# Attention sums with P as the fixed operand, and log-sum loads inside the attention stage

## What is computed

```python
s = jnp.einsum('bnqhd,bnkhd->bnhqk', qb, kk)      # 128 queries x (previous block, own block) of keys
s = jnp.where(mask[None, :, None], s, -jnp.inf)
m = jnp.max(s, axis=-1, keepdims=True)
p = jnp.exp(s - m)
den = jnp.sum(p, axis=-1, keepdims=True)
o = jnp.einsum('bnhqk,bnkhd->bnqhd', p / den, vv)
lse = (m + jnp.log(den))[..., 0]
...
w = jax.nn.softmax(jnp.stack(lses, axis=0), axis=0)   # over the three groups
comb = jnp.einsum('gbsh,gbshd->bshd', w, o)
```

## Time and profile before

| what | us |
|---|---|
| median of 3 runs | 2387.86 (2382.49 to 2400.88) |
| the profiled execution | 2381.88 |
| its span, first to last instruction | 2380.1 |
| TensorE busy | 2281.7 (96%) |
| VectorE busy | 1699.8 (71%) |
| ScalarE busy | 805.8 (34%) |

### The profile page before, as it was taken

One profiled execution on the slowest core, in us unless ns is written; L12 is line 12 of the kernel. 1 busy time (PEld: TensorE's weight loads), 2 busy tenths in 40 slices (PEclk: granted clock), 3 DMA queues, 4 the chain that ended last, 5 costly groups with the idle time before them and its releaser, 6 DMA issues. The chain is left out here.

```text
span 2380.1 us, 36205 instructions
## 1 busy us (share of the span) xinstructions
PE 2281.7 (96%) x12996; PEld 1840.0 (77%) x12996; DVE 1699.8 (71%) x3313; ACT 805.8 (34%) x1705; POOL 299.4 (13%) x487
## 2 busy tenths in 40 slices
PE   7999999979999999999999999889999899999998
PEld 5788878767788888888878887668778636888887
DVE  6756668757685688888868887788888758556663
ACT  5332222112224422121122233776777524122121
POOL 1000012212210012222221210111111000000000
PEclk9999999999999999999999999999999999999999
DMA  8999999999996667878787888766555397434431
GB/s 263 254 278 333 280 276 271 258 248 272 289 276 211 205 190 225 276 253 276 240 264 226 264 293 300 226 228 204 166 192 177 127 319 297 186 117 162 165 146 65
DMA packets 271184, 553.40 MB, mean 233 GB/s; under 512 B 33392, under 2 KB 60480, under 8 KB 268896
## 3 DMA queue, kind: packets, MB, share of 16 engines
q1 hardware_dynamic: 200688, 358.77, 44.2%
q0 software_dynamic: 58000, 166.36, 26.9%
q10 hardware_dynamic: 12320, 25.96, 3.0%
HBM read 442.60 MB, written 191.50 MB: 266 GB/s over the span
## 5 line engine op out<-in xcount | busy, mean ns | idle before, releaser
L1663 PE MATMUL b_acc<-b_whi,a_hi 128*128 128x512 f32 x1792 | 707.0, 395 | 14.9 <-DVE b_wlo L1319 7.3
L1664 PE MATMUL b_acc<-b_wlo,a_hi 128*128 128x512 f32 x1792 | 701.4, 391 | 0.0
L1665 PE MATMUL b_acc<-b_whi,a_lo 128*128 128x512 f32 x1792 | 701.3, 391 | 0.0
L1069 ACT CAST b_whi<-b_w 128x2048 fp32r<-128x2048 f32 (+1 forms) x127 | 228.8, 1802 | 528.3 <-PE b_acc L1665 369.2
L1663 PEld LDWEIGHTS b_acc<-b_whi,a_hi 128*128 128x128 f32 x1792 | 338.9, 189 | 88.8 <-issue 9.4
L1665 PEld LDWEIGHTS b_acc<-b_whi,a_lo 128*128 128x128 f32 x1792 | 338.6, 189 | 71.2
L1664 PEld LDWEIGHTS b_acc<-b_wlo,a_hi 128*128 128x128 f32 x1792 | 339.0, 189 | 69.2
L1319 DVE TENSOR_TENSOR b_wlo<-b_w,b_whi 128x2048 fp32r<-128x2048 f32 (+1 forms) x127 | 273.1, 2151 | 92.2 <-ACT b_whi L1069 92.1
L1113 ACT ACTIVATE c_sm<-c_sm,c_ends 128x256 f32<-128x256 f32 (+1 forms) x384 | 172.5, 454 | 16.6 <-DVE c_ends L1467 16.1
L1467 DVE CUSTOM_DVE_ANT_0 c_sm<-c_p_s,c_mask 128x256 f32<-128x256 f32 (+1 forms) x384 | 120.4, 361 | 36.6 <-PE c_p_s L1752 35.3
L981 POOL DMA_DIRECT2D a_x<-tm x188 | 108.1, 586 | 259.0 <-DVE sT L1433 182.0
(11 more groups left out here) (374 smaller groups left out, 3491.3 us busy)
## 6 DMA issues: line engine op xcount, KB each, us to landing
b_w<-t SPq DMA_DIRECT2D x64, 1024.0 KB, 8.0
t<-in_w_in POOLq DMA_DIRECT2D x48, 1024.0 KB, 11.2
b_w<-in_w_in SPq DMA_DIRECT2D x47, 1024.0 KB, 7.8
a_x<-tm POOLq DMA_DIRECT2D x167, 256.0 KB, 7.1
tm<-b_st SPq DMA_DIRECT2D x128, 256.0 KB, 7.3
b_ck<-in_cache_kv_w POOLq DMA_DIRECT2D x96, 256.0 KB, 4.8
c_qk<-tm SPq DMA_DIRECT2D x96, 256.0 KB, 3.3
t<-t POOLq DMA_DIRECT2D x16, 1024.0 KB, 12.7
```

The costliest lines, as they stand in the source:

```text
L1069: nc.scalar.copy(whi[:, b % HI_RING, part, 0:w], w_raw[:, k, part, 0:w]).then_inc(w_hi, 1)
L1663: nc.tensor.matmul(out, stat_hi, mov_hi, start=first, stop=False)
L1664: nc.tensor.matmul(out, stat_hi, mov_lo, start=False, stop=False)
L1665: return nc.tensor.matmul(out, stat_lo, mov_hi, start=False, stop=last)
```

## The change

`sums` takes P's transpose (128 keys x 128 queries) as the fixed operand and V's 64 columns of the head as the moving one. The output of a task then has queries in the partitions and the 8 heads' 512 columns in a row; `p_o` is [128, 512]. ScalarE copies it to `og` directly. `oT`, `o_move` and the transposes back are gone. `ends_copy` stays at its step, `o_store` moves to the same step. Eleven of the twelve `load_lse` go from SP's list behind the attention into its loop over steps, seven steps after the last unit's scores of the tasks concerned (two steps more for each further load of the two groups whose tasks finish early), each after a wait for the store; the twelfth stays.

```diff
-        p_o = pb("c_p_o", [P, 4, P])
+        p_o = pb("c_p_o", [P, CH])
...
+                lse_at = {}
+                for g in range(3):
+                    of = [i for i, x in enumerate(tasks) if x.g == g]
+                    for n in range(3 if g == 0 else 4):
+                        last = of[4 * n + 3] if g == 0 else of[-1]
+                        lse_at.setdefault(last_unit(last).q // 2 + 7 + (2 * n if g else 0), []).append((g, 4 * n, last))
...
+                    for g, t, last in lse_at.get(s, ()):
+                        for k in range(2):
+                            sp.wait_ge(og_out[k], 16 * ((last - k) // 2 + 1))
+                        late_lse(g, t)
...
-                    if i >= 1:
-                        act.wait_ge(o_moved, i)
-                    nc.scalar.copy(oT[:, :, :], p_o[:, :, :]).then_inc(o_evacd, 1)
+                    if i >= 2:
+                        act.wait_ge(og_out[i % 2], 16 * (i // 2))
+                    nc.scalar.copy(og[:, i % 2, 0:CH], p_o[:, :]).then_inc(o_evacd, 1)
...
-                    act.wait_ge(o_moved, i + 1)
+                    act.wait_ge(o_evacd, i + 1)
...
-                    if q in turn_o_at:
-                        ends_copy(turn_o_at[q])
-                    if q - 2 in turn_o_at:
-                        o_store(turn_o_at[q - 2])
+                    if q - 2 in sum_at and sum_at[q - 2][1].c == 3:
+                        ends_copy(sum_at[q - 2][1].i)
+                        o_store(sum_at[q - 2][1].i)
...
-                def o_move(i):
-                    dve.wait_ge(tqk_done, tqk_no[i, 2])
-                    if i >= 2:
-                        dve.wait_ge(og_out[i % 2], 16 * (i // 2))
-                    V.tensor_copy(og[:, i % 2, 0:CH], p_qk[:, :]).then_inc(o_moved, 1)
...
-                    for b in ((1,) if near else (0, 1)):
-                        n = x.i if b else tasks[x.i].prev
-                        for h in range(2):
-                            cols = slice((2 * x.c + h) * HD, (2 * x.c + h + 1) * HD)
-                            last = nc.tensor.matmul(p_o[HD * h:HD * (h + 1), x.c, :], v[:, n % KEPT, cols],
-                                                    pT[:, x.u % 2, 2 * h + b, :], start=(b == 1 if near else b == 0),
-                                                    stop=(b == 1))
+                    for h in range(2):
+                        cols = slice((2 * x.c + h) * HD, (2 * x.c + h + 1) * HD)
+                        for b in ((1,) if near else (0, 1)):
+                            n = x.i if b else tasks[x.i].prev
+                            last = nc.tensor.matmul(p_o[:, cols], pT[:, x.u % 2, 2 * h + b, :], v[:, n % KEPT, cols],
+                                                    start=(b == 1 if near else b == 0), stop=(b == 1))
...
-                    if q in turn_o_at:
-                        transposes(turn_o_at[q], 2)
...
-        def load_lse():
-            for t in range(0, NT, 4):
-                for g in range(3):
-                    sp.dma_start(lse[:, t:t + 4, g, :], OG[:, g, CH:].rearrange("(t p) c -> p t c", p=P)[:, t:t + 4, :]
-                                 ).then_inc(lse_in, 16)
+        def load_lse(g, t):
+            sp.dma_start(lse[:, t:t + 4, g, :], OG[:, g, CH:].rearrange("(t p) c -> p t c", p=P)[:, t:t + 4, :]
+                         ).then_inc(lse_in, 16)
...
-            load_lse()
+            load_lse(0, NT - 4)
```

More of the change, by code:

```diff
@@ L212, in plan_phase @@
         sb("m_weights", [P, (160160 - 147872) // 4])
-        B["og"], B["ends"], B["oT"] = sb("c_og", [P, 2, OG_W]), sb("c_ends", [P, 4, 2 * NH]), sb("c_oT", [P, 4, P])
+        B["og"], B["ends"] = sb("c_og", [P, 2, OG_W]), sb("c_ends", [P, 4, 2 * NH])
     return B
@@ L450, in project @@
     turn_q_at = {units[4 * i].q - 6: i for i in range(N_TASK)}
-    turn_o_at = {units[4 * i].q + 8: i for i in range(N_TASK)}
     turn_kd_at = {at + 2: n for n, at in t_at.items()}
-    turn_at = sorted((q, place, (i, a)) for a, place, of in ((1, 5, turn_k_at), (0, 5, turn_q_at), (2, 1, turn_o_at),
-                                                          (3, 3, turn_kd_at)) for q, i in of.items())
+    turn_at = sorted((q, place, (i, a)) for a, place, of in ((1, 5, turn_k_at), (0, 5, turn_q_at), (2, 3, turn_kd_at)) for q, i in of.items())
     tqk_no = {what: n + 1 for n, (_, _, what) in enumerate(turn_at)}
-    turned_first = {what: [sum(1 for i, a in tqk_no if a == kind and tqk_no[i, a] < n) for kind in range(4)]
+    turned_first = {what: [sum(1 for i, a in tqk_no if a == kind and tqk_no[i, a] < n) for kind in range(3)]
                     for what, n in tqk_no.items()}
@@ L479, in project @@
         key_of = lambda u: early_keys[key_at[u]] if u < units_early else ck[:, key_at[u], :]
-        qk, v, qT, kT, sm, pT, og, ends, oT = [B[k] for k in ("qk", "v", "qT", "kT", "sm", "pT", "og", "ends", "oT")]
+        qk, v, qT, kT, sm, pT, og, ends = [B[k] for k in ("qk", "v", "qT", "kT", "sm", "pT", "og", "ends")]
         sb("m_projection", [P, (186656 - 24992) // 4])
@@ L540, in project @@
         pt_done, pv_done, o_evacd, o_turned = sem("c_pt_done"), sem("c_pv_done"), sem("c_o_evacd"), sem("c_o_turned")
-        pt_evacd, o_moved = [sem("c_pt_evacd_act"), sem("c_pt_evacd_dve")], sem("c_o_moved")
+        pt_evacd = [sem("c_pt_evacd_act"), sem("c_pt_evacd_dve")]
         turns_ = sem("c_turns")
@@ L554, in attention_over @@
             eng.wait_ge(o_turned, N_TASK)
-            eng.wait_ge(o_moved, N_TASK)
+            eng.wait_ge(o_evacd, N_TASK)
             for k in range(2):
@@ L853, in _ @@
                     block_load_at.setdefault(form_over[n % NFORM], []).append(k)
-                SP_END = max(LATE // 2 + 6, *qk_load_at, *v_load_at) + 1
-                late_tail, late_tile, late_main = ending.sync(sp)
+                lse_at = {}
[4 more added lines that the diff above has]
+                        lse_at.setdefault(last_unit(last).q // 2 + 7 + (2 * n if g else 0), []).append((g, 4 * n, last))
+                SP_END = max(LATE // 2 + 6, *qk_load_at, *v_load_at, *lse_at) + 1
+                late_tail, late_tile, late_main, late_lse = ending.sync(sp)
                 sp.dma_start(lnw[:, :], A["ln_w"]).then_inc(const_in, 16)
@@ L1165, in kd_evac @@
                 def kd_evac(n):
-                    act.wait_ge(tqk_done, tqk_no[n, 3])
+                    act.wait_ge(tqk_done, tqk_no[n, 2])
                     if n >= 1:
@@ L1576, in attend @@
                 def attend(q):
-                    for x in score_at.get(q, ())[0:1]:
-                        mask_and_max(x)
-                    if q in turn_o_at:
-                        o_move(turn_o_at[q])
-                    for x in score_at.get(q, ())[1:2]:
+                    for x in score_at.get(q, ()):
                         mask_and_max(x)
@@ L1715, in transposes @@
                 def transposes(i, a):
-                    for done, n in zip((q_evacd, k_evacd, o_moved, kd_evacd), turned_first[i, a]):
+                    for done, n in zip((q_evacd, k_evacd, kd_evacd), turned_first[i, a]):
                         if n:
@@ L1720, in transposes @@
                         pe.wait_ge(h_dve, N_CONV)
-                    if a == 3:
+                    if a == 2:
                         pe.wait_ge(keyed_g, i + 1)
@@ L1725, in transposes @@
                     else:
[L1726 to L1729, removed]
+                        pe.wait_ge(qk_in[i % 2], 32 * (i // 2) + 32)
                         for c in range(4):
-                            y = oT[:, c, :] if a == 2 else qk[:, i % 4, a, c * P:(c + 1) * P]
-                            last = nc.tensor.transpose(p_qk[:, c * P:(c + 1) * P], y, ident[:, :])
+                            last = nc.tensor.transpose(p_qk[:, c * P:(c + 1) * P], qk[:, i % 4, a, c * P:(c + 1) * P], ident[:, :])
                     last.then_inc(tqk_done, 1)
@@ L1858, in attend @@
                     if q in turn_kd_at:
-                        transposes(turn_kd_at[q], 3)
+                        transposes(turn_kd_at[q], 2)
                     for x in turn_p_at.get(q, ()):
@@ L1905, in _ @@
                     attend(q)
-                pe.wait_ge(o_moved, N_TASK)
+                pe.wait_ge(o_evacd, N_TASK)
                 late_main()
@@ L2292, in main @@
                 sp.wait_ge(stored[k], 16 * (len(range(k, TILES, 2)) + (k == LAST % 2)))
-        return tail, tile, main
+        return tail, tile, main, load_lse
     def gpsimd(pool):
```

## The result

| kernel | median, us | ratio to the kernel before |
|---|---|---|
| before | 2387.86 (2381.27 to 2400.88, 7 runs) | 1 |
| after | 2411.36 (2406.82 to 2416.59, 7 runs) | 1.009 [1.0068, 1.0111] |

The change makes the kernel slower by 0.9%: +21.5 us by the ratio, +23.5 by the medians. The middle is just under 1%; the interval reaches from 0.7 to 1.1%, so these runs do not settle on which side of 1% the change lies. The forecast was 2401 us with a range of 2381 to 2422: the time lies inside, 10 us above it.

The account below looks back on a forecast made before the run. TensorE was taken to bound the attention stage nearly one for one, except in four gate stretches. 67.6 - 27.8 - 9.6 - 12 - 5 = +13.2 us on 2387.9 gave 2401 us, range 2381 to 2422.

Parts of the forecast that it names:

- P fixed, V moving: Attention sums on TensorE: 1200 instructions go from 0.0547 to 0.111 us each, +67.6 us; lower bound +18.4.
- tile shape: Between sums and P's transposes: same shape now, so 0.1 us less at each of 96 bursts, -9.6 us.
- The row of the recurrence's products: Profile row of matmuls with 128 fixed, 64 moving columns, 0.110 us each; taken as pace for the new sums.
- rival (A): Attention sums: moving columns alone set the pace, 0 to +18.4 us, say +9; kernel faster at 2360 us; chance 0.13.
- Turning back: Attention, between scores and sums: four transposes per task vanish, 48 x 0.58 us, -27.8 us.
- those stretches: Four parts of the attention stage where gate blocks load VectorE and ScalarE; TensorE idles 24.8 us there.
- Waits that shrink: Four gate stretches of attention: TensorE waits less for scores' minima and exponentials, -12 us, bounds 0 and -25.
- Log-sum loads: SP's queue behind attention: eleven of twelve loads move into the loop, -5 us, bounds 0 and -12.
- Rival (B): Gate stretches: TensorE's waits stay and the late stage gives nothing, +30.2 us, 2418 us; chance 0.24.
- its own line: Test for the rival of staying waits: it decides once waits and log-sum loads together give less than 6.3 us.
- its own bound of 25: Attention stage: 15 to 20 us growth expected; growth over 25 us would mean wrong in the main.

Follow-up runs that it names:

- E4: Changed kernel with each product of the sums moving 128 columns of V instead of 64; 2407.03 us, 1.0075 of the kernel before.
- E3: Changed kernel with V's columns fixed again and outputs stored turned, the turning back left out of the computation; 2372.04 us, 0.9934 of the kernel before.
- E2: Kernel before with eleven log-sum loads moved into the attention loop, sums as they were; 2380.98 us, 0.9967 of the kernel before.
- E1: Changed kernel with all twelve log-sum loads behind the attention, as before the change; 2418.78 us, 1.0124 of the kernel before.
- E9: Changed kernel with VectorE's and ScalarE's five wide gate operations per block cut to 64 of 512 columns; 2389.52 us, 1.0038 of the kernel before.
- E10: Kernel before with eleven log-sum loads moved and both engines' wide gate operations cut to 64 of 512 columns; 2360.67 us, 0.9908 of the kernel before.
- E8: Changed kernel with only VectorE's five wide gate operations per block cut to 64 of 512 columns; 2405.81 us, 1.0078 of the kernel before.

## Why the prediction was right in its class and 10 us low

- **P fixed, V moving: +67.6 us, right by its pace.** The sums' loads last 192 ns (190 expected), 16 of them take 2.00 us (1.9). From the first sum to P's transposes it is 1710.92 - 1709.08 = 1.84 us, where it was 1704.17 - 1703.14 = 1.03: +0.81 a burst of 16, and the terms for pace and tile shape give 16 x 0.0563 - 0.1 = 0.80. The row of the recurrence's products was the right neighbour, and E4 shows what rival (A) disputed: 64 or 128 moving columns, the pace is the same. Of the Trainium skill, "TensorEngine Tiling (Array Packing)", section "When to Use Tiling", the runs agree with the rule that a fixed operand of at most 64 columns should be packed: from E3 to the changed kernel, packed to unpacked, the runs grow by 37 us.
- **Turning back -27.8, tile shape -9.6: right as work, wrong as time by themselves.** TensorE's busy time falls by 23.1 us in E3 and the intervals of 0.2 and 0.1 us between bursts came as forecast. But the sentence "what TensorE gains or loses in this stage moves its end nearly one for one, except in those stretches" holds for the net change from the load of the kernel before upward, and not below it. Taken alone, the removal gives 8 us in the runs, 14 in the stage. Together with the longer sums it came out at its size: 67.6 - 27.8 - 9.6 = 30.2, measured 29 (E2 to after), 30 (E1) and 31 us (E9 to E10).
- **Waits that shrink: -12, the term that failed.** The prediction gave two reasons: VectorE's copy is gone, and TensorE's part grows, which leaves the other engines time. Idle time did fall, 36.5 to 26.3 us in the stage, 24.8 to 18.0 in the stretches (some 13 expected), but the stage did not become shorter by it: there TensorE's busy time grew by 40.8 us and not by 30.2, and 40.8 - 10.2 = 30.6. In the runs too the net is the 29 to 31 us of the bare sum. At the clock of the kernel before, in E4 against E2, idle falls by only 3.7 us (39.9 to 36.2) with the stage 23.4 longer; by the runs 1.0075 / 0.9967 is 26 us. The rest of the fall in idle time is a slower TensorE that waits less and gains nothing. E8 and E9 show that ScalarE's gate work has a part in the waits too, while the removed copies lay on VectorE; how the waits divide between the two engines is not shown.
- **The clock was not in the sum.** The granted clock fell from 0.97 to 0.93 in the stage; E4 gives it back by wider moving parts alone. Net price: 3.6 us by the runs, within their uncertainty, 6.7 in the profiled stage.
- **Log-sum loads: -5, measured -8.** E1 and E2 give 8.1 and 7.9 us from both sides, inside the bounds of 0 and -12; that the two agree so closely is chance. The 11 loads in the loop cost the attention nothing (stage 420.5 in E2). In the profiled pair of before and after only 1.9 us of it shows between last store and output stage (76.5 to 74.6), in E2's profile 5.4; single executions differ by such amounts. The prediction called the time of the twelve loads "otherwise half-idle"; by bytes it was (157 against 391 GB/s), but the DMA engines are busy there at a share of 0.84.
- **Rival (B)** said that the waits stay and that the late stage gives nothing. The first half is nearer to the runs than the forecast's -12, the second half fell with E2. By its own line, waits and loads together under 6.3 us, it did not win: 30.2 - 21.5 = 8.7 us, nearly all of it from the loads.
- **The sum.** 30.2 (form) - 3.7 (waits at the old clock) + 3.6 (clock) - 8 (log-sums) = +22 us; measured +21.5. The prediction had +13.2: 8 too much for waits and 4 for the clock left out, 3 too little for the loads. The terms are uncertain by several us each, so the close agreement of the sum is partly luck. So is the class: in the stage alone the prediction had 67.6 - 27.8 - 9.6 - 12 = +18.2 us, the profiles show 30.6 (and 450.8 - 420.5 = 30.3 between E1 and E2), past its own bound of 25. What brought the whole back to 0.9% is the gain of the loads.

## What to carry over

An f32 product with 64 fixed columns, packed two by two, is not worth trading for one with 128 fixed and 64 moving columns to save transposes: here the pace went from 0.055 to 0.112 us an instruction, 68 us in the prediction's sum, against 37 us of transposes and changes of tile shape saved; the runs show a net loss of 29 us. A wait that shrinks is a gain only at an unchanged clock, so read idle time, busy time and granted clock of a stage together. And find out which engine holds the wait by cutting its work, as E8 and E9 do, before you count the work that the edit happens to take off one of them. And look at the two parts of a change apart: the loads moved off a late queue were the half that is worth keeping (E2, 0.9967).

## What the runs showed of the hardware

- The f32 product with 128 fixed columns starts every 0.11 us with 64 and with 128 moving columns (2.00 us for 16 in both), and each load lasts 192 ns. At a granted clock of 0.50 the same 16 take 3.67 us.
- With the wide and the narrow moving part the pace is the same and the granted clock is not: whole-kernel means of 0.978 with 64 and 0.984 with 128 moving columns, the stage 0.93 and 0.98, with the same number of instructions. The narrow part is not the only thing that lowers it: E3, with the old sums, has a mean of 0.9785 (0.976 to 0.981), and E9, narrow but with short gates, 0.983 (0.980 to 0.985). What TensorE did before each fall to 1.2 GHz was not taken apart further, and the cause stays open; idle time alone does not explain it, for E4 idles more (36.2 us) than the changed kernel (26.3) at the higher clock.
- Twelve loads of 64 bytes a row in one series hold SP's queue for 13.2 to 14.0 us, 1.1 to 1.2 each; the single one that is left in the changed kernel holds it for 0.46.
